# A sine asked for one pair later, and a setup spread by one count over three layers

## The reference, cut to what matters

```python
x = x + g2 * sqrelu_mlp(hl2, w_mlp1, w_mlp2)      # first block, w_mlp1: 2048 x 8192
...
proj = hn @ w_in                                  # second block: conv_a, conv_gate, ssm_u, 1024 columns each
lam = lax.complex(lam_re, lam_im)
dt = jnp.exp(log_dt)[:, None]
lam_bar = jnp.exp(lam * dt)
b_bar = ((lam_bar - 1.0) / lam)[..., None] * b
_, states = lax.associative_scan(combine, (a, bu), axis=1)
```

## Time and profile before

| | |
|---|---|
| median of 3 runs | 4369.22 us |
| lowest, highest | 4367.89, 4374.9 us |
| the profiled execution | 4375.66 us |
| its span | 4373.9 us |
| PE, busy | 3928.3 us (90%) |
| DVE, busy | 2817.6 us (64%) |
| ACT, busy | 2062.4 us (47%) |
| POOL, busy | 203.9 us (5%) |
| L207, DVE, the splits | 2240 of 696 ns, 1527.7 us |
| L200, ACT, the roundings | 2240 of 630 ns, 1389.0 us |

### The profile page before, as it was taken

One profiled execution on the slowest core, in us unless ns is written; L12 is line 12 of the kernel. 1 busy time (PEld: TensorE's weight loads), 2 busy tenths in 40 slices (PEclk: granted clock), 3 DMA queues, 4 the chain that ended last, 5 costly groups with the idle time before them and its releaser, 6 DMA issues. The chain is left out here.

```text
span 4373.9 us, 65273 instructions
## 1 busy us (share of the span) xinstructions
PE 3928.3 (90%) x21628; PEld 3227.4 (74%) x21628; DVE 2817.6 (64%) x5302; ACT 2062.4 (47%) x3817; POOL 203.9 (5%) x242
## 2 busy tenths in 40 slices
PE   6799968667999999898889998998799999999998
PEld 0467744556888888776678877877688888888887
DVE  0553345677777666759586557688866666666667
ACT  0442320135555555455545434444865555555554
POOL 3011100000000000002110000000000000000000
PEclk9899979888999999998999999999999999999999
DMA  9686720024666665451155535555156666666664
GB/s 340 229 302 248 267 61 0 1 81 147 196 198 198 191 191 188 151 170 68 49 164 178 181 112 168 166 187 182 53 155 205 204 203 187 187 191 189 188 190 160
DMA packets 199376, 735.03 MB, mean 168 GB/s; under 512 B 22903, under 2 KB 22936, under 8 KB 197400
## 3 DMA queue, kind: packets, MB, share of 16 engines
q1 hardware_dynamic: 173992, 639.97, 46.4%
q0 software_dynamic: 25200, 92.64, 5.8%
HBM read 715.74 MB, written 16.78 MB: 167 GB/s over the span
## 5 line engine op out<-in xcount | busy, mean ns | idle before, releaser
L207 DVE TENSOR_TENSOR weights_lo<-ring,weights_hi 128x512 fp32r<-128x512 f32 x2240 | 1527.7, 696 | 1018.8 <-ACT weights_hi L200 1005.3
L200 ACT ACTIVATE weights_hi<-ring 128x512 fp32r<-128x512 f32 x2240 | 1389.0, 630 | 1309.8 <-PE ps L846 1244.6
L846 PE MATMUL ps<-expert_parts,weights_hi 128*128 128x512 f32 x4224 | 1467.0, 395 | 34.3 <-DVE weights_lo L207 26.8
L846 PE MATMUL ps<-expert_parts,weights_lo 128*128 128x256 f32 x4224 | 1141.4, 280 | 0.0
L846 PEld LDWEIGHTS ps<-expert_parts,weights_hi 128*128 128x128 f32 x4224 | 780.8, 189 | 205.8 <-issue 36.4
L846 PEld LDWEIGHTS ps<-expert_parts,weights_lo 128*128 128x128 f32 x4224 | 797.2, 189 | 20.4
L846 PE MATMUL ps<-mlp_parts,weights_hi 128*128 128x512 f32 x1024 | 361.5, 397 | 37.6 <-DVE weights_lo L207 21.8
L846 PE MATMUL ps<-hidden,weights_hi 128*128 128x512 f32 x1024 | 351.5, 392 | 0.6 <-DVE weights_lo L207 0.6
L846 PE MATMUL ps<-h_parts,weights_hi 128*128 128x512 f32 x704 | 269.5, 410 | 10.0 <-DVE weights_lo L207 10.0
L846 PE MATMUL ps<-mlp_parts,weights_lo 128*128 128x256 f32 x1024 | 277.0, 281 | 0.0
L846 PE MATMUL ps<-hidden,weights_lo 128*128 128x256 f32 x1024 | 275.9, 280 | 0.0
(11 more groups left out here) (454 smaller groups left out, 5071.7 us busy)
## 6 DMA issues: line engine op xcount, KB each, us to landing
ring<-in_w_mlp SPq DMA_DIRECT2D x256, 512.0 KB, 3.6
ring<-in_w_u SPq DMA_DIRECT2D x256, 512.0 KB, 3.9
ring<-in_w_v_tab SPq DMA_DIRECT2D x256, 512.0 KB, 3.6
ada_ring<-in_w_ada POOLq DMA_DIRECT2D x124, 512.0 KB, 6.4
ring<-in_w_mix SPq DMA_DIRECT2D x88, 512.0 KB, 5.2
ada_ring<-in_w_ada SPq DMA_DIRECT2D x68, 512.0 KB, 5.2
ring<-in_w_out SPq DMA_DIRECT2D x64, 512.0 KB, 3.6
ring<-in_w_in SPq DMA_DIRECT2D x48, 512.0 KB, 3.6
```

Source lines behind the costliest of these rows:

```text
L200: act.activation(core.hi[:, g % SLOTS], core.ring[:, slot, at:at + QUARTER], ACT.Copy).then_inc(core.rounded, 1)
L207: dve.tensor_tensor(core.lo[:, g % SLOTS], core.ring[:, slot, at:at + QUARTER], core.hi[:, g % SLOTS].bitcast(F32), ALU.subtract).then_inc ...
L846: mm = pe.matmul(out, part[:, g % SLOTS, k, :], moving, start=at == 0 and part is core.hi, stop=last and part is core.hi)
```

## The change

The sine of pair u is taken in the take of tile 2u + 2, before the phases of pair u + 1 are made; the last pair's sine stays at tile 63. And `after_split` gets the quarter's number counted from the start of the stage's first layer.

```diff
@@ linear_stage, run
                     def make_layer(core, dve, g, i, per, base):
                         make_lo(core, dve, g, i, per, base)
-                        layer.beside.after_split(dve, i * per + g)
+                        layer.beside.after_split(dve, layer.Q - layers[0].Q + i * per + g)
@@ class TurnsBeside
+    def sine(self, act, u):
+        act.wait_ge(self.done["phase"], u + 1)
+        act.activation(self.trig[:, u % 2], self.trig[:, u % 2], ACT.Sin, scale=TWO_PI).then_inc(self.done["trig"], 1)
+
     def scalar(self, act, turns):
         n, small = turns[0], self.core.small
         u = n // 2
-        if n % 2 == 0 and 0 <= u < PAIRS:
+        if n % 2 == 0 and u < PAIRS:
             if u == 0:
                 act.wait_ge(self.done["rate"], 1)
+            else:
+                self.sine(act, u - 1)
             if u >= 2:
                 act.wait_ge(self.kept[u % 2], 16 * (u // 2))
             turn = self.turn[:, u:u + 1]
@@
-        if n % 2 == 1 and 0 <= u < PAIRS:
-            act.wait_ge(self.done["phase"], u + 1)
-            act.activation(self.trig[:, u % 2], self.trig[:, u % 2], ACT.Sin, scale=TWO_PI).then_inc(self.done["trig"], 1)
+        if n == 2 * PAIRS - 1:
+            self.sine(act, PAIRS - 1)
```

## The result

The changed kernel takes 4323.63 us (median of 4, 4321.49 to 4326.77), the kernel before in the same rounds 4372.06 us (median of 4, 4367.89 to 4375.34): a ratio of 0.9893, 95% interval 0.988 to 0.9905. It is 48.4 us faster; the forecast was 44.3 us and 4325. The profiled execution took 4325.26 us, with a span of 4323.5.

What follows compares the result with a forecast made beforehand. PE was taken as the bound, with holes at the sines and the end of in2. -28.7 - 21.1 + 5.5 = -44.3 us from 4369.2 gave 4325 us, range 4316 to 4342.

Steps and rivals of the forecast that it cites:

- Part 1, the sine: Beside the first MLP layer, the later sine ends 31 stalls of 0.925 us: 28.7 us gained.
- Part 2, the end of in2: At the end of in2, the new count leaves no setup to run alone: 21.1 us gained.
- (a): In2, quarters 48 to 51, tile 12: setup steps and the reciprocal delay DVE's splits, 2.4 us lost.
- (b): In2, the tile behind the new PE hole runs at the 1.2 GHz level: 1.5 us lost.
- (c): In2, tiles 13 to 15: splits carry setup steps and DVE falls behind, 0.2 us lost at quarter 64.
- (d): In2, quarter 68: a budget of five setup steps falls due at once, 1.1 us lost.
- (e): In2, quarters 69 to 76: nine setup steps, 0.3 us lost until arrears are gone.
- The stall did not become another: Rival, 10%: beside the sines DVE's reserve is too thin, first split late by half of today's; 4339 us.
- The setup did not cost 12 us: Rival, 12%: setup steps cost 12 us inside in2; 4331 us.
- The count spreads the setup: Rival, 3%, claimed the opposite: part of the setup steps stays at in2's end; 4340.5 us with part 1 alone.
- PE did not stay at 1.2 GHz: Rival, slower, 2%: in in2 PE drops to 1.2 GHz at (a)'s hole and stays there; 4388 us.
- The table switch: Rival, 4%: each ACT table load stalls another 1283 ns, PE loses about 1 us once at tile 2; 4326 us.

Runs made afterwards that it cites:

- e5: The changed kernel with one added 256-column DVE addition, its result unread, before each pair's phase subtractions; 4325.37 us, ratio 0.9894 to the kernel before.
- e6: The changed kernel with two added 256-column DVE additions, results unread, before each pair's phase subtractions; 4336.13 us, ratio 0.9918 to the kernel before.
- e7: The kernel before, unchanged, run once more for a second profile; 4371.59 us.
- e2: The kernel before with only the new quarter count over all layers, the sine asked in its old place; 4352.65 us, ratio 0.9964.
- e0: The changed kernel, unaltered, measured again; 4323.26 us, ratio 0.9891 to the kernel before.
- e10: The changed kernel, unaltered, measured again beside the study's best version on one chip; 4318.64 us, 49.3 us below the kernel before.
- e1: The changed kernel with the quarter count of before, so the later sine alone; 4339.61 us, ratio 0.9931 to the kernel before.
- e3: The changed kernel with the setup's second half from quarter 36 at 400 columns a quarter, not 48 at 650; 4323.09 us, ratio 0.9894.

## Why the prediction was right, step by step

The forecast was a gain of 44.3 us; the medians gave 48.4, and the stages 47.8. Below I go by the stages.

**Part 1, the sine: 28.7 us forecast, 28.51 measured.** 31 stalls of 0.925 us went and the one of the last pair stayed (3.3 us, one wait). The odd tile's reserve, 0.3 us by the burst's times, is 0.39 by e5 and e6. The even tile costs nothing: behind the sine and the phases ACT's roundings run in a burst (1237.35), and PE stays at 40.00 of 40. The first table load left no mark that I can tell from zero.

**Part 2, the end of in2: 21.1 forecast, 21.05 measured.** The 27 steps were over at 1908.78 + 0.68, five tiles before the stage's end. The 1.9 us that I expected from the last sum to the next stage were a slip against my own sum, 21.87 - 21.1 = 0.8; it is 0.82.

**The cost inside in2: 5.5 forecast, 5.16 measured, and term by term.** The terms can be read from the distances between the first matmuls of PE's tiles, in us, which are 5.57 where nothing disturbs. Tile 12's start is 1863.44 and tile 13's 1872.84 in the changed kernel's rows above; the others are worked out from the traces.

| tiles | before again (e7) | changed | difference | forecast |
|---|---|---|---|---|
| 12 | 7.06 | 9.40 | 2.34 | (a) 2.4 |
| 13 | 5.57 | 6.95 | 1.38 | (b) 1.5 |
| 14 to 16 | 16.70 | 16.89 | 0.19 | (c) 0.2 |
| 17, quarters 68 to 71 | 5.57 | 6.63 | 1.06 | (d) 1.1 |
| 18 and 19 | 11.13 | 11.33 | 0.19 | (e) 0.3 |

What carried (a) is DVE's chain. From the first split of tile 12 to the split that PE needs for tile 13 the walk gave 1901.6 - 1891.35 = 10.25 us; in the trace PE's first matmul of tile 13 starts 1872.84 - 1862.61 = 10.23 behind that split. ACT's wait for the sum behind the reciprocal shows it as well:

```profile
1871.04 0.42 ACT L2401 ACTIVATE in_sums<-in_sums 128x256 f32<-128x256 f32 x1 [5.33 <-DVE in_sums L816]
```

What failed is the state of PE in between. The forecast let PE run tile 12 at 1.2 GHz as in rows 10 and 11, which left a hole of 2.4 us. PE ran it at the full clock, was done 1.2 us earlier, and waited 3.60 for the same split. So DVE sets the time at which tile 13 starts, and whatever PE gains before it is given back as a longer wait. e2 and e5 show the other case: there the clock fell at tile 12, the hole before tile 13 is 2.16 and 2.03 us, and tile 12 takes the same 9.39 and 9.40. Their tile 13 takes 7.22 and 7.21, not 6.95, and in2 133.85 and 133.86, 0.25 more than in the changed kernel. The price of (d), 1.06 us for the tile, is more than its hole of 0.79, which stands behind the five steps from 1894.67 to the split at 1898.29. Terms (c) and (e) cost their few tenths without a hole that the rows name.

**What was left out: 3.5 us.** The mixer gives 1.65: the forecast had it as an allowance of 2 us in its low end, not in its middle, though rows 7 showed that the wait ahead of it would go. And its reason was half right: PE does open the mixer at the full clock, which gains nothing, and the gain is a fall of the clock 14 us later that does not come. The stretch behind the sines gives 1.10 in both kernels with the later sine, by the granted clock (0.84 against 0.82); why the clock falls for less time there is open. Some 0.65 us more come in the later stages. 0.58 of it, between splits 852 and 1200, repeats in three traces of the changed kernel (607.26 to 607.29), but neither part alone has it (608.14, 608.11), so it is no price of an edit. The three make 3.4. With the 0.34 too much that I had for in2, less the 0.19 + 0.05 too much at the two gains, that is the difference. Each of the forecast's own terms is within 0.2 us of what was measured.

**The rivals.** The stall did not become another; DVE has 0.39 us of room, and e6 shows what would have come of it, 0.29 us a pair for 0.68 of work, 9.6 us in all. The setup did not cost 12 us. The count spreads the setup (e2 alone gains its 21.05). PE did not stay at 1.2 GHz: in the window from 1873 to 1875 it is at 0.50, and the hole at quarter 69, 26 us later, finds it at full speed (the matmul behind it takes 0.50 us, not 0.77). The table switch: ACT's own rows in the changed kernel have a load between two activations.

```profile
1857.21 0.42 ACT L2401 ACTIVATE in_sums<-in_sums 128x256 f32<-128x256 f32 x1 [0.82 <-DVE in_sums L816]
1857.64 1.28 ACT L1684 ACT_TABLE_LOAD   x1
1858.94 0.23 ACT L1684 ACTIVATE s_r<-s_r 128x32 f32<-128x32 f32 x1
```

The sigmoid ends at 1857.63, the load starts at 1857.64 and ends at 1858.92, and the exponential starts at 1858.94, so a switch costs ACT 1.3 us. The Trainium skill's page "ScalarE: Activation LUTs", section "What ACT_TABLE_LOAD costs", adds about 1380 ns of drain to each switch. These rows leave no room for it, so here the measurement decides.

## What to carry to other kernels

Where two engines hand work to each other in one tile, ask for the answer a tile later and price the gain by the period of undisturbed tiles, not by the length of the wait: ACT waited 3.2 us a pair and PE lost 0.925. When work is spread under a stage, walk the busiest queue instruction by instruction to the point where the next engine has to wait; that time holds even where the clock of the engine that waits comes out otherwise, while the length of its hole does not. And start such a spread away from the tile that is late already: where to begin and what else stands in front of that tile was worth 6.9 us here, more than the whole price of the spread.

## What the runs showed of the hardware that was not expected

The same hole of 2.43 us before tile 12 of in2 brought PE's clock down in some traces (both of before, e2, e5) and not in others (the changed kernel, e0, e10, e1, e6). It cost 1.4 us: tile 12 takes 7.06 us in e7 and 5.63 in e1, which do the same work there. It repeats from one execution of a kernel to the next, twice for before and three times for the changed kernel. It also goes with the stretch between splits 740 and 760 ahead of it: where the clock fell at tile 12, that stretch had a granted clock of 0.82 or 0.79, and where it didn't, 0.84. What links the two was not tested, and e3 stands outside of it: with 0.84 there and a further hole at tile 10, its clock fell behind the hole of 2.44 us (tile 12 takes 7.21).

The saves of the sines land in 2.6 us where the sine is asked for early (before, e7, e2) and in 4.4 to 5.4 (medians; up to 6.3) where it comes a tile later (all the others). It is off the path: two tiles, 11.1 us, lie between a sine and the next use of its buffer, and ACT's list of waits has none for a save. What delays it was not tested.

The first 970 us vary by up to 12 us between executions of any kernel here. An effect of 3 to 4 us is lost in the medians of four to seven runs, and shows within hundredths in the distance between two named instructions of one engine.
